# The start of a one-core encoder kernel: GpSimd's low parts of a token pair's sums wait for VectorE's scales and weight splits

## The chip, the cores and the metric

The kernel runs on one core of a Trainium2 chip. The metric is the device time of one execution in microseconds (us). TensorE is called PE here, VectorE DVE, ScalarE ACT, GpSimd POOL, SyncE SP, as in the rows of the profile.

## What is computed

A one-layer encoder over 1280 tokens (a sequence of 256 and one of 1024) of width 1024, in float32:

```python
x = x + 0.5 * swiglu(rmsnorm(x, norm_ffn1), w_ffn1_gate, w_ffn1_up, w_ffn1_down)   # d_ff 2816
x = x + hybrid_mixer(rmsnorm(x, norm_mix), ...)       # windowed attention and gated linear attention
x = x + 0.5 * swiglu(rmsnorm(x, norm_ffn2), w_ffn2_gate, w_ffn2_up, w_ffn2_down)
y = rmsnorm(x, norm_final)
```

Only the first RMSNorm and the first gate product matter for this change. `rmsnorm(x, g)` is `x * rsqrt(mean(x*x) + 1e-6) * g`.

## The kernel before

All float32 products are made of three matmuls on split operands: a high part, rounded to the type that PE multiplies, and a low part, which is the value less its high part (high by high, high by low, low by high). The gate and up products use a seven-product scheme for 2 by 2 blocks (GP1 to GP7), so PE needs not only the four blocks of the normalized tokens but also four sums of blocks, t1 to t4 (they feed GP5, GP6, GP7 and GP4).

At the beginning the 1280 tokens are ten tiles of 128, taken as five pairs (tile t and tile t+5). `PAIR_ORDER[0]` is 0, 1, 2, 3, 4. For each pair i this pipeline runs, each engine going through its own hand-written list strictly in order, with semaphores between engines:

- ACT, `norm_squares` (L1111): the sum of squares of each tile. POOL, `norm_roots` (L980, L983): two small instructions for each tile that turn it into the scale factor.
- DVE, `norm_scales` (L1580): tokens by factor by gain, one instruction of 128x1024 for each tile. PE, `norm_turn` (L2126): 8 transposes for each tile into PSUM.
- ACT, `norm_blocks` (L1123 to L1127): four evictions. DVE, `norm_blocks` (L1592 to L1613): seven instructions of 128x512, which are the sums t1 to t4 into `first_t` (L1601, L1606, L1608, L1613) and three low parts of blocks (L1592), all with one input in PSUM.
- ACT, `norm_sums` (L1133): the high part of each sum. POOL, `norm_t_lo` (L994): its low part, one instruction of 128x512 on two SBUF inputs for each sum, t1 to t4. They count on the semaphore `t_low`.

There is one set of t1 to t4 for all pairs. So DVE's `norm_blocks` of pair i may write sum j only when POOL has read it for pair i-1:

```python
def t_free(j):
    if i:
        dve.wait_ge(t_low[f], 4 * (i - 1) + j)
```

Between these stand the preparations of the first weight blocks, `g_prepare(0, s)` on DVE: the low part of weight block s (L1623, counted on `B["lo"]`) and, for s = 0 and s = 2, sums of weight blocks (L1636, L1638, L1642, counted on `B["summed"]`: 2 after s = 0, 3 after s = 2), all with two inputs in SBUF. DVE's list is: scales of pairs 0 and 1, blocks 0, scales 2, prepare 0, blocks 1, scales 3, prepare 1 and 2, blocks 2, scales 4, prepare 3 and 4, blocks 3, three evictions of gate products, blocks 4, and then the steady loop. ACT's list is: squares 0 and 1, then for each i blocks i, squares i+2, sums i, and after the sums its part of the same weight blocks (L1153); after the sums of pair 3 it evicts the first gate product (`first_p`, L1163). POOL's list is: roots 0, 1, 2, then for each i the low parts of pair i and the roots of pair i+3.

PE's list is: transposes of pairs 0 to 3, gate products 0, 1 and 2 over pairs 0 to 2 (columns c = 0), transposes of pair 4, the other products. Transposes of pair 3 wait for the end of DVE's blocks 2, those of pair 4 for the end of blocks 3. Product GP6 (step 1, c = 0) waits for POOL's second low part of pair 2, and GP2 (step 2) for ACT's eviction of GP1:

```python
if f == 0 and i >= 2:
    pe.wait_ge(N["lo"], 7 * max(1, i if i > 2 else 1))
```

SP loads x and the first three weight units at the very beginning; a later weight load waits until DVE has counted a weight block (L576).

Of the kernel before, what the change touches and what calls it, by code (L numbers as in the profile page):

```python
# [87 lines left out]
HT = TT // 2  # L88
# [61 lines left out]
def build(nc, x_prompt, x_sample, norm_ffn1, w_ffn1_gate, w_ffn1_up, w_ffn1_down, norm_mix, w_in, attn_sink,  # L150
# [4 lines left out]
    with ctx:  # L155
# [183 lines left out]
        def h_piece(f, j, e, pair):  # L339

            if f == 0:
                return hs[:, j, e, pair, :]
            if pair < 2:
                return hs2_first[:, 2 * j + e, pair, :]
            return hs2_last[:, pair - 2, :] if j + e == 0 else hq[:, 3 * (2 * j + e - 1) + pair - 2, :]
# [76 lines left out]
        def named(prefix, names):  # L422
            return {k: sem(f"{prefix}_{k}") for k in names.split()}
# [7 lines left out]
        B = named("block", "summed hi lo")  # L431
# [530 lines left out]
        def _(pool):  # L962
# [13 lines left out]
            def root(n, t, at=None):  # L976
                N = NORMS[n]
                at = t if at is None else at
                pool.wait_ge(N["sum"], at + 1)
                nc.gpsimd.tensor_scalar(ssq[:, n, t:t + 1], ssq[:, n, t:t + 1], EPS, 1.0, ALU.add, ALU.mult  # L980
                                        ).then_inc(N["root"], 1)
                pool.wait_ge(N["root"], 2 * at + 1)
                nc.gpsimd.tensor_tensor(rstd[:, n, t:t + 1], ssq[:, n, t:t + 1], expo[:, 0:1], ALU.pow  # L983
                                        ).then_inc(N["root"], 1)

            def norm_roots(f, i):
                for e in range(2):
                    root(2 * f, N_TILES[f][2 * i + e], 2 * i + e)

            def norm_t_lo(f, i):  # L990
                pair = PAIR_ORDER[f][i]
                for j, b in enumerate((GP5, GP6, GP7, GP4)):
                    pool.wait_ge(NFF[f]["hi"], 8 * i + 4 + j + 1)
                    nc.gpsimd.tensor_tensor(h_piece(f, b, 1, pair), SUMS[f][j + 1][:, :], h_piece(f, b, 0, pair).bitcast(F32),  # L994
                                            ALU.subtract).then_inc(t_low[f], 1)

            for i in range(3):
                norm_roots(0, i)
            for i in range(HT):
                norm_t_lo(0, i)  # L1000
                if i + 3 < HT:
                    norm_roots(0, i + 3)

            def g_gate(f, s, c):
                q, j = divmod(s, NP)
# [56 lines left out]
            for i in range(HT):  # L1062
                norm_roots(1, i)
                if i:
                    norm_t_lo(1, i - 1)
            norm_t_lo(1, HT - 1)
            for s, c in GORDER:
                g_gate(1, s, c)
# [1523 lines left out]
```

## Time and profile before

| what | us |
|---|---|
| median of 3 runs | 2313.0 (2310.67 to 2313.32) |
| the profiled execution | 2310.25 |
| its span | 2308.3 |
| TensorE clock granted, mean | 0.987 of full |

The span begins with the first instruction; what is around it is 1.95 us. The stretch that the change touches is the first 65 us of the span. The profile's timeline gives for each instruction, or run of like instructions, the start, the time and in brackets how long the engine sat idle before it and for whom. The windows view gives busy time of each engine within a stretch and the granted PE clock (1.00 is 2.4 GHz, 0.50 is 1.2 GHz).

### The profile page before, as it was taken

How to read it: one execution, taken by the hardware profiler on the slowest of the kernel's cores; microseconds unless marked ns; L12 is line 12 of the kernel's file. 1: busy time of each engine (PE TensorE's matmuls, PEld its weight loads, DVE VectorE, ACT ScalarE, POOL GpSimd, SP SyncE). 2: the span in 40 equal slices, each digit the busy share in tenths (PEclk: the TensorE clock that was granted, in tenths of full speed). 3: DMA queues.
4: the chain of work that ended last, by engine and by line, in shares of the span. 5: the costliest groups of instructions: out<-in, count | busy, mean ns of one | idle time of the engine just before them, and what ended most of it. 6: DMA issues, size and time to landing. Idle time of an engine off the chain costs nothing. (4 is left out here: it accounts for less than half of the span.)

```text
span 2308.3 us, 35188 instructions
## 1 busy us (share of the span) xinstructions
PE 2225.7 (96%) x13488; PEld 2004.7 (87%) x13488; DVE 1422.6 (62%) x2373; ACT 812.0 (35%) x1566; POOL 313.7 (14%) x296
## 2 busy tenths in 40 slices
PE   4999999999999999999999989899999999999998
PEld 3999999999888887776778767799999999988887
DVE  7655565565575776665655774765555555557576
ACT  6323222222333446544442211532322222233343
POOL 5100011000100002100011222521111111110000
PEclk7999999999999999999999999999999999999999
DMA  3222322322785655523335863122232232277554
GB/s 129 79 93 77 95 90 88 108 81 77 272 267 166 201 159 149 177 63 99 97 105 154 252 200 100 73 80 92 77 95 89 89 108 82 78 275 264 166 191 167
DMA packets 247141, 306.10 MB, mean 133 GB/s; under 512 B 24128, under 2 KB 159808, under 8 KB 246976
## 3 DMA queue, kind: packets, MB, share of 16 engines
q1 hardware_dynamic: 236608, 282.88, 38.7%
q10 hardware_dynamic: 10368, 20.98, 2.4%
q8 instruction: 109, 1.79, 0.3%
q14 instruction: 56, 0.46, 0.1%
HBM read 209.43 MB, written 91.10 MB: 130 GB/s over the span
## 5 line engine op out<-in xcount | busy, mean ns | idle before, releaser
L2162 PE MATMUL ps<-hs,w_hi 128*128 128x384 f32 (+1 forms) x1232 | 380.6, 309 | 3.6 <-DVE first_u L1671 2.1
L2163 PE MATMUL ps<-hs,w_hi 128*128 128x384 f32 (+1 forms) x1232 | 380.1, 309 | 0.0
L2164 PE MATMUL ps<-hs,w_lo 128*128 128x384 f32 (+1 forms) x992 | 306.1, 309 | 0.0
L2172 PE MATMUL ps<-w_hi,dh 128*128 128x512 f32 x770 | 300.7, 390 | 2.0 <-DVE w_lo L1725 0.8
L2174 PE MATMUL ps<-w_hi,dh 128*128 128x512 f32 x770 | 299.7, 389 | 0.0
L1623 DVE TENSOR_TENSOR w_lo<-w_raw,w_hi 128x512 fp32r<-128x512 f32 x178 | 133.3, 749 | 179.1 <-ACT w_hi L1153 176.7
L2173 PE MATMUL ps<-w_lo,dh 128*128 128x512 f32 x610 | 237.3, 389 | 0.0
L2162 PEld LDWEIGHTS ps<-hs,w_hi 128*128 128x128 f32 x1232 | 233.1, 189 | 4.5 <-issue 4.5
L1153 ACT CAST w_hi<-w_raw 128x512 fp32r<-128x512 f32 x220 | 135.7, 617 | 283.7 <-PE ps L2164 280.9
L2163 PEld LDWEIGHTS ps<-hs,w_hi 128*128 128x128 f32 x1232 | 233.1, 189 | 0.0
L1722 DVE TENSOR_TENSOR dh<-dr,dh 128x640 fp32r<-128x640 f32 x154 | 126.8, 824 | 167.5 <-ACT dh L1184 167.4
L1184 ACT CAST dh<-dr 128x640 fp32r<-128x640 f32 x154 | 112.0, 727 | 281.3 <-PE ps L2174 259.9
L2163 PE MATMUL ps<-hq,w_hi 128*128 128x384 f32 x616 | 206.2, 335 | 0.0
L2164 PEld LDWEIGHTS ps<-hs,w_lo 128*128 128x128 f32 x992 | 187.6, 189 | 0.0
L2162 PE MATMUL ps<-hq,w_hi 128*128 128x384 f32 x528 | 177.1, 335 | 0.8 <-DVE second_u L1671 0.8
L2162 PE MATMUL ps<-hs_first,w_hi 128*128 128x256 f32 x616 | 174.0, 282 | 3.8 <-DVE hq_f L1566 2.8
L2163 PE MATMUL ps<-hs_first,w_hi 128*128 128x256 f32 x616 | 174.2, 283 | 0.0
L2172 PEld LDWEIGHTS ps<-w_hi,dh 128*128 128x128 f32 x770 | 144.5, 188 | 33.4 <-DVE dh L1722 1.6
L2174 PEld LDWEIGHTS ps<-w_hi,dh 128*128 128x128 f32 x770 | 144.5, 188 | 30.1
L2093 PE MATMUL ps<-h_hi,w_hi 128*128 128x512 f32 (+1 forms) x432 | 161.7, 374 | 4.7 <-ACT q_rot L1266 2.5
L2095 PE MATMUL ps<-h_hi,w_lo 128*128 128x512 f32 (+1 forms) x432 | 154.2, 357 | 0.0
L2094 PE MATMUL ps<-h_lo,w_hi 128*128 128x512 f32 (+1 forms) x432 | 154.2, 357 | 0.0
(259 smaller groups left out, 4621.1 us busy)
## 6 DMA issues: line engine op xcount, KB each, us to landing
dr<-hid_mid SPq DMA_DIRECT2D x154, 320.0 KB, 3.3
w_raw<-in_w_ffn_down SPq DMA_DIRECT2D x176, 256.0 KB, 3.5
hid_mid<-st SPq DMA_DIRECT2D x88, 320.0 KB, 2.2
w_raw<-in_w_ffn_gate SPq DMA_DIRECT2D x44, 512.0 KB, 5.2
w_raw<-in_w_ffn_up SPq DMA_DIRECT2D x44, 512.0 KB, 5.1
hid_mid<-sg SPq DMA_DIRECT2D x66, 320.0 KB, 2.2
hq<-o_mid SPq DMA_DIRECT2D x60, 128.0 KB, 3.3
w_raw<-in_w_in SPq DMA_DIRECT2D x14, 512.0 KB, 4.9
```

Source lines behind the costliest of these rows:

```text
L1153: nc.scalar.copy(g_block(s)[0], src).then_inc(B["hi"], 1)
L1623: v.tensor_tensor(lo, src, hi.bitcast(F32), ALU.subtract).then_inc(B["lo"], 1)
L1722: v.tensor_tensor(a_lo, DR[f][n % D_HID][:, :], a_hi.bitcast(F32), ALU.subtract).then_inc(W["a_lo"], 1)
L2093: mm(out, hi, rhs_hi, start=first, stop=False)
L2094: mm(out, hi, rhs_lo, start=False, stop=False)
L2095: return mm(out, lo, rhs_hi, start=False, stop=last)
L2162: mm(out, hi[:, k, :], b_hi, start=k == 0 and j in (GP1, GP6, GP5), stop=False, skip_group_check=True)
L2163: mm(out, hi[:, k, :], b_lo, start=False, stop=False, skip_group_check=True)
L2164: last = mm(out, lo[:, k, :], b_hi, start=False, stop=k == 3, skip_group_check=True)
L2172: mm(out, hi, w_h, start=first and p in D_FRESH, stop=False, skip_group_check=True)
L2173: mm(out, hi, w_l, start=False, stop=False, skip_group_check=True)
L2174: return mm(out, lo, w_h, start=False, stop=last, skip_group_check=True)
```

## The change

Two things, both in POOL's list, both for the first norm only. For pairs 0, 1 and 2 `norm_t_lo` now first waits until DVE has prepared weight block 0, 2 or 4 (with its sums), that is, until just before DVE's blocks 1, 2 and 3. And the roots run one pair further ahead: roots 0 to 3 stand before the low parts of pair 0, and roots i+4 follow the low parts of pair i. No instruction is added or removed, and no other engine's list changes.

```diff
             def norm_t_lo(f, i):
                 pair = PAIR_ORDER[f][i]
+                if f == 0 and i < 3:
+                    pool.wait_ge(B["lo"], (1, 3, 5)[i])
+                    pool.wait_ge(B["summed"], (2, 3, 3)[i])
                 for j, b in enumerate((GP5, GP6, GP7, GP4)):
                     pool.wait_ge(NFF[f]["hi"], 8 * i + 4 + j + 1)
                     nc.gpsimd.tensor_tensor(h_piece(f, b, 1, pair), SUMS[f][j + 1][:, :], h_piece(f, b, 0, pair).bitcast(F32),
                                             ALU.subtract).then_inc(t_low[f], 1)
 
-            for i in range(3):
+            for i in range(4):
                 norm_roots(0, i)
             for i in range(HT):
                 norm_t_lo(0, i)
-                if i + 3 < HT:
-                    norm_roots(0, i + 3)
+                if i + 4 < HT:
+                    norm_roots(0, i + 4)
```

## Rows read from the trace of the kernel before

**Rows 1.** The page, part 1: busy time, share of the span, instructions

```profile
PE 2225.7 (96%) x13488; PEld 2004.7 (87%) x13488; DVE 1422.6 (62%) x2373; ACT 812.0 (35%) x1566; POOL 313.7 (14%) x296
```

**Rows 2.** Windows: stretch, its length, busy time by engine, PEclk, DMA share, GB/s

```profile
core 0: us, PE busy (x) PEld busy (x) DVE busy (x) ACT busy (x) POOL busy (x), PEclk, DMA share, GB/s
46.40:48.48 2.08, 2.08 (x9) 2.08 (x8) 2.08 (x4) 1.65 (x4) 0.00 (x0) 0.50 0.02 4
48.48:51.80 3.32, 3.32 (x19) 3.00 (x18) 3.32 (x6) 1.84 (x3) 2.08 (x2) 1.00 0.00 0
57.00:64.00 7.00, 7.00 (x51) 7.00 (x48) 5.30 (x9) 4.80 (x10) 4.47 (x4) 1.00 0.00 0
```

**Rows 3.** Waits of PE in 0 to 75 us: total, times, longest

```profile
PE ps L2126 <- DVE hs L1592: 16.4, 1, 16.4
PE ps L2162 <- ACT first_p L1163: 1.5, 2, 1.4
```

**Rows 4.** Timeline of DVE, 0 to 75 us: start, time, line, idle before

```profile
14.64 1.28 DVE L1580 SCALAR_TENSOR_TENSOR hs_f<-hs_f,rstd 128x1024 f32<-128x1024 f32 x1 [0.72 <-POOL rstd L983]
...
20.03 4.59 DVE L1580 SCALAR_TENSOR_TENSOR hs_f<-hs_f,rstd 128x1024 f32<-128x1024 f32 x2
24.55 1.76 DVE L1623 TENSOR_TENSOR w_lo<-w_raw,w_hi 128x512 fp32r<-128x512 f32 x1
26.23 1.75 DVE L1636 TENSOR_TENSOR w_sum<-w_raw 128x512 f32<-128x512 f32 x1
28.01 0.69 DVE L1638 TENSOR_TENSOR w_sum<-w_sum,w_raw 128x512 f32<-128x512 f32 x1
28.62 0.68 DVE L1601 TENSOR_TENSOR first_t<-first_t,ps 128x512 f32<-128x512 f32 x1
...
32.81 4.22 DVE L1580 SCALAR_TENSOR_TENSOR hs_f<-hs_f,rstd 128x1024 f32<-128x1024 f32 x2
...
42.95 4.24 DVE L1580 SCALAR_TENSOR_TENSOR hs_f<-hs_f,rstd 128x1024 f32<-128x1024 f32 x2
...
48.32 0.67 DVE L1601 TENSOR_TENSOR first_t<-first_t,ps 128x512 f32<-128x512 f32 x1
...
51.91 0.67 DVE L1592 TENSOR_TENSOR hs<-ps,hs 128x512 fp32r<-128x512 f32 x1
...
71.45 0.69 DVE L1636 TENSOR_TENSOR w_sum<-w_raw 128x512 f32<-128x512 f32 x1 [3.10 <-DMA w_raw<-in_w_ffn_up]
```

**Rows 5.** Timeline of POOL, 0 to 75 us

```profile
20.06 7.37 POOL L994 TENSOR_TENSOR hs<-first_t,hs 128x512 fp32r<-128x512 f32 x4
...
30.03 5.92 POOL L994 TENSOR_TENSOR hs<-first_t,hs 128x512 fp32r<-128x512 f32 x4
...
38.73 0.19 POOL L980 TENSOR_SCALAR ssq<-ssq 128x1 f32<-128x1 f32 x1
39.00 0.56 POOL L983 TENSOR_TENSOR rstd<-ssq,expo 128x1 f32<-128x1 f32 x1
...
49.72 5.01 POOL L994 TENSOR_TENSOR hs<-first_t,hs 128x512 fp32r<-128x512 f32 x4 [3.62 <-ACT hs L1133]
59.53 5.05 POOL L994 TENSOR_TENSOR hs<-first_t,hs 128x512 fp32r<-128x512 f32 x4 [4.79 <-ACT hs L1133]
```

**Rows 6.** Timeline of ACT, 0 to 75 us

```profile
25.81 0.19 ACT L1111 ACTIVATION_READ_ACCUMULATOR junk<-hs_f 128x1 f32 x1
...
38.03 0.19 ACT L1111 ACTIVATION_READ_ACCUMULATOR junk<-hs_f 128x1 f32 x1
...
45.99 0.59 ACT L1123 COPY first_t<-ps 128x512 f32<-128x512 f32 x1 [1.88 <-PE ps L2126]
...
52.54 0.47 ACT L1163 COPY first_p<-ps 128x384 f32<-128x384 f32 x1
```

**Rows 7.** Timeline of PE, 0 to 110 us

```profile
43.08 3.68 PE L2126 MATMUL ps<-ident,hs_f 128*128 128x128 f32 x16 [16.43 <-DVE hs L1592]
46.41 0.67 PE L2162 MATMUL ps<-hs,w_hi 128*128 128x384 f32 x1
...
53.16 0.41 PE L2162 MATMUL ps<-hs,w_hi 128*128 128x384 f32 x1 [1.36 <-ACT first_p L1163]
```

**Rows 8.** Waits of SP's queue, 0 to 110 us

```profile
SPq L576 <- DVE w_lo L1623: 66.3, 3, 47.5
```

## The prediction

> **What bounds the kernel now.** I read the page's part 1 first: PE is busy 96% of the span [rows 1], so what an edit is worth is read from PE's own idle stretches. The waits of PE over the first 75 us come next. The longest is 16.4 us, in which the transposes of pair 3 wait for the end of DVE's blocks 2, and a short one of 1.36 us follows, for ACT's `first_p` [rows 3, 7]. The timelines say what that wait is made of. DVE runs without a gap from its blocks 0 to the end of blocks 3 at 52.58 [rows 4], PE starts pair 3 at 43.08 [rows 7], just when DVE's blocks 2 are done (the scales behind them start at 42.95 [rows 4]), and PE starts GP2 at 53.16 [rows 7], when ACT's `first_p` of 52.54 is done [rows 6]. After that PE is busy all the time, 7.00 of 7.00 us from 57 to 64 [rows 2]. So up to about 53 us DVE's list is the critical path, and behind it PE is. What counts is how late PE's GP2 starts; that delay is carried to the end as it is.
>
> **What the change takes away.** Where DVE's two-input SBUF work lies beside POOL's low parts, both are slow. Two scales take 4.59, 4.22 and 4.24 us, while one beside nothing but small work takes 1.28 [rows 4]; with the usual overlap of 0.08 between neighbours, two take 1.20 + 1.28 = 2.48. The first weight split and the first weight sum take 1.76 and 1.75, where the next sum takes 0.69 [rows 4]. POOL's four low parts take 7.37 and 5.92 us there, and 5.01 where DVE does only blocks (49.72) [rows 5]. With every overlap gone DVE would save 2.11 + 2.14 (scales 2, block 0) + 1.74 + 1.76 (scales 3 and 4) = 7.75 us. Seven block instructions, with an input in PSUM, take 32.81 - 28.62 = 4.19 us [rows 4] whether POOL works or not, so POOL's new place costs them no speed.
>
> **What the change adds.** POOL's low parts of pair i now lie wholly beside DVE's blocks i+1, and these write the very sums that POOL still reads (`t_free`). Before, POOL was done or nearly so. Now DVE's t1 must wait for POOL's first, t4 for POOL's fourth. From POOL's start to the end of DVE's blocks it is then 5.01 us for the four (1.25 each), 0.04 for a semaphore, t4 0.60 and the last low part 0.68: 6.3 us, where DVE alone needs 4.19 + 0.08. And POOL can start later than DVE's list arrives, because the roots of the pair four ahead now stand in front of the low parts on POOL's queue; they need ACT's squares. What is queued behind the waiting POOL instruction is its own three further low parts and the next roots. DVE's blocks wait for the low parts and DVE's scales for the roots; ACT waits for neither, but its casts of the sums and `first_p` follow DVE's blocks.
>
> The schedule, instruction by instruction, from durations of rows 4 to 7:
>
> *Round 1.* Scales 2 start at 20.03 as now and end at 22.51; block 0 with its two sums takes to 24.43 (now 28.70). ACT is not touched so far, so its last square of pair 3 comes at 25.81 + 0.19 = 26.00 [rows 6]. POOL then does a root, 0.19 + 0.56 with gaps [rows 5], to 26.90. Its four low parts run from 26.93 to 31.94. DVE's blocks 1 end at 33.26. The scales behind them start at 33.18, now 32.81: later by 0.37. All that was gained (4.25) and more is spent in waiting from 24.43 to 28.23 for the first low part and between the sums.
>
> *Round 2.* ACT's casts follow DVE's t4, so the squares of pair 4 end 0.37 later than 38.22 [rows 6], at 38.59. DVE does scales 3 in 2.48 and three weight instructions and is ready at 37.46. POOL does the roots to 39.49 and only then starts pair 1's low parts: 39.52 to 44.53. Blocks 2 end at 45.85, the next starts at 45.77, now 42.95 [rows 4]: later by 2.82.
>
> *Round 3.* No roots stand here. Scales 4 and two weight splits take 2.40 + 1.20 + 0.08 from 45.77, to 49.45; POOL's wait ends there, its low parts run from 49.50 to 54.51, and blocks 3 end at 55.83, now 52.58 [rows 4]: later by 3.25. PE's pair 3 starts at 45.90, ACT's copies of it at 48.8 (2.91 behind PE, as 45.99 is behind 43.08 [rows 6, 7]), which is before POOL's first low part at 50.76 and so decides nothing. GP1 follows PE's transposes by 3.33, at 49.23, and with GP6 it takes 5.4 us, 46.41 to 51.80 now [rows 2, 7], so to 54.6. GP6, the second half of that, needs POOL's second low part of pair 2, out at 52.0: in time. ACT's last cast and then `first_p` move with DVE's t4, to an end of 56.25, and GP2 starts at 56.40 in place of 53.16: **3.24 us later**.
>
> *Behind it.* Pair 3's low parts on POOL go from 54.5 to 59.6, before pair 4's, which were at 59.53 with 4.79 of idle time in front [rows 5] and move to 62.8; nothing is added. Nothing absorbs the 3.24 either: the next weight loads are issued when DVE has counted a block (SP waited 66.3 us in all at L576 for DVE [rows 8]), and so DVE's wait of 3.10 us for such a load at 71.45 [rows 4] moves along with everything else. I take 3.2 us as the whole effect.
>
> Bounds: if POOL's four take 5.92 [rows 5] as with one neighbour slow, each of three rounds is 0.9 longer, and 3.2 becomes 5.9. On the other side, what I take for semaphore gaps and the order of the small roots could be 0.3 less a round, which gives 2.3. I take the fast figure since 49.72 has DVE in exactly the work that will stand beside it.
>
> **Rivals.** *The overlap alone counts (faster).* If POOL's start didn't hold DVE, the list would be shorter by up to 7.75 us: 2313.0 - 7.75 = 2305.3. For it speaks that DVE is without a gap now; against it stands that the waits are in DVE's code and that ACT's squares come at 26.00 and 38.22 whatever DVE does. It decides at POOL's first low part: it would have to start by about 23.3, and a root before it needs a square of 26.00. The Trainium skill, page "SBUF — State Buffer", section "SBUF: two separate sides", calls the pair of ports that DVE and POOL share an exclusive lock, held for the whole instruction. By that rule each of DVE's eight two-input instructions would be held once for a whole low part of 1.25 us, which makes the gain 10.0 and this rival 2303.0; the rows lie below that, with 7.75.
>
> *PE's clock stays low (slower).* PE runs at 0.50 (1.2 GHz) up to 48.48 and at 1.00 (2.4 GHz) behind it, 5.4 us after the transposes of pair 3 began [rows 2, 7]. PE stands idle for 2.8 us longer now, and between GP6 and GP2 for 1.8 in place of 1.36. If the rise comes only after GP2 has begun, a matmul costs twice the 0.175 us (19 in 3.32 [rows 2]) that it takes at the full clock. The 24 matmuls of GP1 and GP6 then take 8.4 us from 49.2 and end at 57.6, 1.2 after GP2 would start, and GP2 with its 12 costs 2.1 more: 3.2 + 1.2 + 2.1 = 6.5 us, 2319.5. It decides at 56.4. Against it: a rise 5.4 us after 45.9 is at 51.3, and the gap of 1.36 us in the trace did not bring the clock down.
>
> *The change does nothing.* If the counts that POOL now waits for were always there, 2313.0 would stay. They aren't: POOL starts at 20.06, the count comes at 24.43.
>
> **How the numbers follow.** The profiled execution took 2310.25 us, span 2308.3 and 1.95 around it; with the change it would take 2313.5. The median of the runs is 2.75 above it, and the difference goes on top of the median: 2313.0 + 3.2 = 2316.2. Chances: this forecast 0.80 (with its bounds 2.3 to 5.9), clock rival 0.07, overlap rival 0.04, nothing 0.04, the rest for something unseen. 0.2% is 4.6 us, about what a measurement can tell from no change. The forecast lies within it, with a spread of runs of 2.65 us; a quarter of its weight falls over the line. So: faster 0.05, same 0.70, slower 0.25. The range takes the bounds 2.3 and 5.9 and some 1.3 of spread on each side: 2314.0 to 2320.2; I widen the lower end to 2312.8, for the runs' own median may come out lower.
>
> **What would show it.** DVE's scales and first weight split without the slow rows (1.28 and 0.69), DVE idle in front of L1601 for POOL's L994 in blocks 1 (near 3.8 us), 2 (near 3.4) and 3 (near 1.3), and idle between the sums; POOL's L994 at 26.9, 39.5 and 49.5 with 5.0 us for four; PE's L2126 of pair 3 at 45.9 and GP2 at 56.4. Wrong it would be if POOL's low parts take other than 1.25 beside blocks, if DVE's blocks 2 end before 43, or if PE's idle time behind 57 us shrinks by what came in front.

## The result and the profile after

| | before | after |
|---|---|---|
| median of 20 runs | 2312.2 us (2309.94 to 2319.32) | 2315.55 us (2313.52 to 2320.66) |
| profiled execution, span | 2310.25, 2308.3 | 2314.80, 2312.8 |

The ratio of after to before is 1.0015, with a 95% interval of 1.0009 to 1.0021: some 3.4 us slower (2.1 to 4.9), less than the 0.2% line but clear of zero. 2316.2 had been forecast.

In the changed kernel all lines behind the change stand three lower (L1580 is L1583, L1601 is L1604, L994 is L997, L2126 is L2129, L2162 is L2165). The timeline of DVE answers to rows 4:

```profile
20.08 2.47 DVE L1583 SCALAR_TENSOR_TENSOR hs_f<-hs_f,rstd 128x1024 f32<-128x1024 f32 x2
22.47 0.68 DVE L1626 TENSOR_TENSOR w_lo<-w_raw,w_hi 128x512 fp32r<-128x512 f32 x1
...
27.93 0.69 DVE L1604 TENSOR_TENSOR first_t<-first_t,ps 128x512 f32<-128x512 f32 x1 [3.45 <-POOL hs L997]
...
32.81 2.47 DVE L1583 SCALAR_TENSOR_TENSOR hs_f<-hs_f,rstd 128x1024 f32<-128x1024 f32 x2
...
40.39 0.69 DVE L1604 TENSOR_TENSOR first_t<-first_t,ps 128x512 f32<-128x512 f32 x1 [3.31 <-POOL hs L997]
...
45.27 2.47 DVE L1583 SCALAR_TENSOR_TENSOR hs_f<-hs_f,rstd 128x1024 f32<-128x1024 f32 x2
...
50.35 0.69 DVE L1604 TENSOR_TENSOR first_t<-first_t,ps 128x512 f32<-128x512 f32 x1 [1.40 <-POOL hs L997]
...
54.69 0.68 DVE L1595 TENSOR_TENSOR hs<-ps,hs 128x512 fp32r<-128x512 f32 x1
```

All three pairs of scales take 2.47 now, in place of 4.59, 4.22 and 4.24 [rows 4], and the first split 0.68 in place of 1.76. In front of each of the three blocks DVE now sits idle for POOL: 3.45, 3.31 and 1.40 us. Compare where the scales start. Scales 3 start at 32.81, to the hundredth where they started before; scales 4 at 45.27 in place of 42.95; blocks 3 end at 55.37 in place of 52.58. The timeline of POOL says why, and answers to rows 5:

```profile
26.12 0.55 POOL L983 TENSOR_TENSOR rstd<-ssq,expo 128x1 f32<-128x1 f32 x1
26.64 4.93 POOL L997 TENSOR_TENSOR hs<-first_t,hs 128x512 fp32r<-128x512 f32 x4
...
38.58 0.56 POOL L983 TENSOR_TENSOR rstd<-ssq,expo 128x1 f32<-128x1 f32 x1
39.10 4.93 POOL L997 TENSOR_TENSOR hs<-first_t,hs 128x512 fp32r<-128x512 f32 x4
49.03 9.95 POOL L997 TENSOR_TENSOR hs<-first_t,hs 128x512 fp32r<-128x512 f32 x8 [4.99 <-DVE w_hi L1626]
```

The low parts of pairs 0 and 1 start right behind the last root of the pair ahead (26.12, 38.58), not when DVE has its weight block ready (24.48 and 37.09). Only in round 3, at 49.03, is it the new wait that releases them. PE, and PE's clock in the stretches around GP2 (columns: stretch, its length, PE busy, PEclk, DMA share, GB/s):

```profile
45.41 3.67 PE L2129 MATMUL ps<-ident,hs_f 128*128 128x128 f32 x16 [20.26 <-DVE hs L1595]
...
55.95 0.41 PE L2165 MATMUL ps<-hs,w_hi 128*128 128x384 f32 x1 [1.92 <-ACT first_p L1166]
...
59.67 1.91 PE L2129 MATMUL ps<-ident,hs_f 128*128 128x128 f32 x16
```

```profile
54.00:56.00 2.00, 0.08 (x2) 1.00 0.00 0
56.00:58.00 2.00, 2.00 (x7) 0.56 0.03 8
58.00:60.00 2.00, 2.00 (x10) 0.59 0.00 0
60.00:62.00 2.00, 2.00 (x19) 1.00 0.00 0
```

GP2 starts at 55.95, 2.79 later than before [rows 7]. But then, in this execution, PE's clock is at 1.2 GHz for most of 56 to 60, after an idle time of 1.92 us; GP2 takes 3.72 us until pair 4's transposes begin at 59.67. In the trace of before these began at 55.32, 2.16 behind GP2. So this one pair of profiles shows 2.79 of DVE's list and 1.56 of clock, 4.35 us, at pair 4. First and last start of a down product on PE, in before and then in after:

```profile
L2172 PE MATMUL ps<-w_hi,dh x770: 387/389/500, 594.9 to 2300.3; 128*128 128x512 f32 x193
```

```profile
L2175 PE MATMUL ps<-w_hi,dh x770: 387/389/498, 599.5 to 2304.7; 128*128 128x512 f32 x193
```

4.6 at the beginning of the down products, 4.4 at their end: in this pair no later stage gives any of it back. The medians lie only 3.4 apart; a second pair of profiles, below, bears on that.

### The profile page after: what moved, and what is told of

Read it like the earlier page. It is cut to its first block and busy times, and to the rows that moved or that the text cites. A ratio compares the mean times of both kernels' runs of the same rounds, so it can differ in the third digit from the quotient of the medians.

```text
span 2312.8 us, 35191 instructions
## 1 busy us (share of the span) xinstructions
PE 2225.9 (96%) x13488; PEld 2005.1 (87%) x13488; DVE 1415.9 (61%) x2373; ACT 811.8 (35%) x1566; POOL 308.2 (13%) x296
## 5 line engine op out<-in xcount | busy, mean ns | idle before, releaser
L2165 PE MATMUL ps<-hs,w_hi 128*128 128x384 f32 (+1 forms) x1232 | 381.1, 309 | 4.6 <-DVE first_u L1674 2.2
L2165 PEld LDWEIGHTS ps<-hs,w_hi 128*128 128x128 f32 x1232 | 233.2, 189 | 5.9 <-issue 5.8
L2165 PE MATMUL ps<-hq,w_hi 128*128 128x384 f32 x528 | 177.1, 335 | 0.8 <-DVE second_u L1674 0.8
L2165 PE MATMUL ps<-hs_first,w_hi 128*128 128x256 f32 x616 | 174.1, 283 | 3.8 <-DVE hq_f L1569 2.8
```

What stands on the lines that cost most here:

```text
L2165: mm(out, hi[:, k, :], b_hi, start=k == 0 and j in (GP1, GP6, GP5), stop=False, skip_group_check=True)
```

## The experiments

The theory: the waits free DVE of the overlap, as meant, but DVE may not write the one set of sums before POOL has read it; and the roots that were put ahead of POOL's low parts hold these back by another 2 us in the first two rounds. Rivals: the waits alone are the cost; the roots cost nothing; the fall of PE's clock is the cost.

| run | GP2 on PE starts | idle before | pair 4 starts | ratio to before (95%) |
|---|---|---|---|---|
| before, two profiles | 53.16, 53.29 | 1.36, 1.48 | 55.32, 55.45 | 1 |
| after, two profiles | 55.95, 56.04 | 1.92, 1.84 | 59.67, 58.23 | 1.0015 (1.0009 to 1.0021) |
| waits only | 52.46 | 1.93 | 54.65 | 0.9994 (0.9985 to 1.0003) |
| roots only | 56.94 | 3.48 | 60.92 | 1.0020 (1.0011 to 1.0029) |
| first wait only | 53.76 | 1.78 | 55.92 | 1.0002 (0.9993 to 1.0011) |
| after, two sets | 49.3 | none | 51.42 | 0.9986 (0.9977 to 0.9995) |
| after, second set for pair 1 | 51.58 | 1.91 | 53.74 | 0.9990 (0.9981 to 0.9998) |
| after, two sets, two waits | 51.34 | 2.87 | 54.95 | 0.9993 (0.9985 to 1.0002) |
| before, two sets | 53.02 | 1.93 | 56.16 | 1.0001 (0.9992 to 1.0010) |
| after, gap filled | 56.2 | filled | 58.37 | 1.0027 (1.0018 to 1.0036) |
| after, 11 matmuls at 33 us | 56.05 | 1.93 | 59.45 | 1.0033 (1.0020 to 1.0045) |

### The waits alone

```diff
+                if f == 0 and i < 3:
+                    pool.wait_ge(B["lo"], (1, 3, 5)[i])
+                    pool.wait_ge(B["summed"], (2, 3, 3)[i])
```

> The three waits of the change, with the roots left where the kernel before has them (three pairs ahead). Theory (the cost comes from POOL's start being held by the roots of the next pair, not from the waits as such): pair 0's low parts start at 24.5 in place of 26.6, blocks 1 end near 30.8, pair 1's low parts start near 35.3, blocks 2 end near 41.6, blocks 3 near 52.0, GP2 starts near 52.5: 0.65 us earlier than before (53.16), time between 2311 and 2312, ratio to before 0.9997. Rival (the waits alone cost, because DVE's blocks are held by POOL's low parts): blocks 3 end 2.8 us later than before, GP2 near 56, ratio 1.0012 or more.

Its DVE, and PE's GP2:

```profile
26.28 0.69 DVE L1604 TENSOR_TENSOR first_t<-first_t,ps 128x512 f32<-128x512 f32 x1 [1.43 <-POOL hs L997]
...
31.16 2.48 DVE L1583 SCALAR_TENSOR_TENSOR hs_f<-hs_f,rstd 128x1024 f32<-128x1024 f32 x2
...
41.75 2.48 DVE L1583 SCALAR_TENSOR_TENSOR hs_f<-hs_f,rstd 128x1024 f32<-128x1024 f32 x2
...
52.46 0.42 PE L2165 MATMUL ps<-hs,w_hi 128*128 128x384 f32 x1 [1.93 <-ACT first_p L1166]
```

DVE waits 1.43, 1.43 and 1.41 us in front of the three rounds' blocks, the time of POOL's first low part (some 1.2) and the semaphores, and another 0.5 between the sums. Scales 3 start 1.65 us before those of after, scales 4 3.5 before. GP2 comes at 52.46 where 52.5 was expected, 0.7 before the kernel before. The ratio, 0.9994, is not clear of 1; it is clear of the rival's 1.0012. The waits as such don't cost: in each round they give about as much as they take.

### The roots alone

Against the kernel before:

```diff
-            for i in range(3):
+            for i in range(4):
                 norm_roots(0, i)
...
-                if i + 3 < HT:
-                    norm_roots(0, i + 3)
+                if i + 4 < HT:
+                    norm_roots(0, i + 4)
```

> The roots one pair further ahead, without the waits. Theory: the roots of pair 3 hold POOL's low parts of pair 0 until 26.6, those of pair 4 hold pair 1's until 39.1, so rounds 1 and 2 are as in the changed kernel (scales 4 at 45.3) and only round 3 has the old overlap back; blocks 3 end near 54.9, GP2 starts near 55.4, 2.3 us later than before, and more where PE's clock falls in the gap; ratio 1.0010 to 1.0017. Rival (the waits cost, the order of the roots nothing): GP2 at 53.2, ratio 1.0000.

The same two engines:

```profile
28.02 0.69 DVE L1601 TENSOR_TENSOR first_t<-first_t,ps 128x512 f32<-128x512 f32 x1 [3.44 <-POOL hs L994]
...
45.36 4.52 DVE L1580 SCALAR_TENSOR_TENSOR hs_f<-hs_f,rstd 128x1024 f32<-128x1024 f32 x2
49.81 1.77 DVE L1623 TENSOR_TENSOR w_lo<-w_raw,w_hi 128x512 fp32r<-128x512 f32 x1
...
56.94 0.66 PE L2162 MATMUL ps<-hs,w_hi 128*128 128x384 f32 x1 [3.48 <-ACT first_p L1163]
```

Up to scales 4 (45.36 against 45.27) this is the changed kernel: the roots hold POOL there whether it waits for DVE or not (its low parts start at 26.73 and 39.19, in the changed kernel at 26.64 and 39.10). Round 3 cost more than I expected, for POOL's low parts of pair 2 now lay beside the scales and also beside a weight split (1.77), so GP2 came at 56.94 and not at 55.4; the gap in front of it grew to 3.48 us, the clock fell and pair 4 came at 60.92. The ratio of 1.0020 is above the 1.0010 to 1.0017 expected, and the rival's 1.0000 is out. Together with the run before this one: the loss of the change is that of its roots.

### A second set of sums

POOL's hold on DVE is taken away by writing t1 to t4 of pairs 1 and 3 elsewhere, into the places of tokens that are already scaled (for pair 3 DVE first waits until all of them are).

```diff
+        SET_B = (1, 3)
...
+        def sums(f, i):
+            return [SUMS[0][0]] + set_b[i] if f == 0 and i in SET_B else SUMS[f]
...
+                if f == 0 and i in (3, 4) and i - (2, 1)[i - 3] in SET_B:
+                    act.wait_ge(t_low[0], 4 * (i - (2, 1)[i - 3]) + 4)
...
-                    if i:
-                        dve.wait_ge(t_low[f], 4 * (i - 1) + j)
+                    if i and (f or i not in SET_B):
+                        last = i - 2 if f == 0 and i - 1 in SET_B else i - 1
+                        dve.wait_ge(t_low[f], 4 * last + j)
+                    elif i == 3:
+                        dve.wait_ge(N["scaled"], 2 * HT)
```

> The changed kernel with a second set of t1 to t4 for pairs 1 and 3 (in the places of tokens already scaled), so that DVE's blocks 1, 2 and 3 need not wait for POOL's low parts of the pair before. Theory (what the change gives in speed of the scales and splits is spent in waiting for the one set of sums): blocks 1 start at 24.4, blocks 2 end near 39, blocks 3 near 47.4, GP2 starts at 48 to 49, that is 4 to 5 us before the kernel before; ratio 0.9980 to 0.9984. Rival (DVE's list is held by the roots or by ACT, not by the sums): GP2 no earlier than 53, ratio 0.9997 or more.

Its DVE, then what now waits for POOL on ACT and on PE:

```profile
24.28 0.68 DVE L1615 TENSOR_TENSOR first_s<-first_t,ps 128x512 f32<-128x512 f32 x1
...
28.46 4.17 DVE L1591 SCALAR_TENSOR_TENSOR hs_f<-hs_f,rstd 128x1024 f32<-128x1024 f32 x2
...
39.61 3.60 DVE L1591 SCALAR_TENSOR_TENSOR hs_f<-hs_f,rstd 128x1024 f32<-128x1024 f32 x2
```

```profile
54.54 0.59 ACT L1134 COPY first_t<-ps 128x512 f32<-128x512 f32 x1 [2.42 <-POOL hs L1003]
```

```profile
47.14 0.41 PE L2176 MATMUL ps<-hs,w_hi 128*128 128x384 f32 x1 [2.01 <-POOL hs L1003]
```

DVE goes on at 24.28 without a wait, scales 4 start 5.7 us before those of after, and pair 4 on PE at 51.42, 3.9 before the kernel before. The overlap is back in part (4.17, 3.60), as POOL's late start now meets the next scales. POOL is the next bound: PE waits 2.01 for it, and ACT 2.42 at the wait that the second set needs; by the product that starts at 73.35 in before and at 71.19 here, 2.2 of the 3.9 are left. The ratio, 0.9986, is just short of the 0.9980 to 0.9984 expected: the mechanism is confirmed, its size was a little too high, since I had left POOL out as the next bound. This is the fastest kernel of the study, 3.3 us under before. It keeps the new order of the roots, and POOL starts pair 0 at 26.85 in it; two sets with the roots where they were was not run.

With the second set for pair 1 alone (`SET_B = (1,)`), one hold is left, that on blocks 3:

> The changed kernel with a second set of t1 to t4 for pair 1 alone, so that DVE's blocks 1 and 2 are free of POOL, and blocks 3 wait for it as in the changed kernel. Theory (the wait for the sums is the price, round by round): scales 4 start near 39.6 as with two sets for both pairs, POOL's low parts of pair 2 start at 44.5, blocks 3 end near 50.8, GP2 near 51.3; ratio 0.9990 to 0.9994. Rival (the gain of the run with two sets came from pair 3): ratio 1.0 or more.

Scales 4 and the start of blocks 3 on its DVE:

```profile
39.79 3.59 DVE L1591 SCALAR_TENSOR_TENSOR hs_f<-hs_f,rstd 128x1024 f32<-128x1024 f32 x2
...
45.98 0.69 DVE L1615 TENSOR_TENSOR first_t<-first_t,ps 128x512 f32<-128x512 f32 x1 [1.39 <-POOL hs L1003]
```

Blocks 3 wait 1.39, as in after, GP2 comes at 51.58 and the ratio is 0.9990: both as forecast.

Without the new waits and roots, the second sets should be worth nothing, because DVE never waited for POOL in the kernel before:

> The kernel before (no new waits, roots three pairs ahead) with the second set of t1 to t4 for pairs 1 and 3. Theory: DVE had no idle time for POOL before, so the second set gives nothing: scales 2, 3 and 4 stay at 4.2 to 4.6 us, blocks 3 end near 52.6, GP2 starts near 53.2, ratio between 0.9995 and 1.0005. Rival (the second set alone brings what the two sets brought with the change, 0.9986): ratio 0.9988 or less, GP2 before 51.

The scales 3 and 4 on its DVE:

```profile
32.63 4.24 DVE L1588 SCALAR_TENSOR_TENSOR hs_f<-hs_f,rstd 128x1024 f32<-128x1024 f32 x2
42.79 4.24 DVE L1588 SCALAR_TENSOR_TENSOR hs_f<-hs_f,rstd 128x1024 f32<-128x1024 f32 x2
```

They are: 1.0001, with GP2 at 53.02. So neither half brings the 0.9986 by itself: the second sets alone give nothing, the waits alone 0.7 us at GP2, and with the new roots they lose.

### Where the overlap goes when one wait is made

Against the kernel before, the waits of the change for pair 0 only, the roots as they were:

```diff
+                if f == 0 and i < 1:
+                    pool.wait_ge(B["lo"], (1, 3, 5)[i])
+                    pool.wait_ge(B["summed"], (2, 3, 3)[i])
```

> The kernel before with the first of the three new waits alone (pair 0's low parts wait for weight block 0 and its sums), roots as before, one set of sums. Theory: the first round gains the most (scales 2 and two weight instructions, 4.2 us) and pays the least (POOL can start at 24.5 to 25.0, right when DVE is ready), so scales 3 start near 31.2 in place of 32.8, and rounds 2 and 3 run as before, 1.6 us earlier; GP2 near 51.5, ratio 0.9991 to 0.9995. Rival (each round pays what it gains): GP2 near 53, ratio 0.9998 or more.

Its DVE from scales 3 to scales 4, blocks 2 left out:

```profile
30.70 3.49 DVE L1583 SCALAR_TENSOR_TENSOR hs_f<-hs_f,rstd 128x1024 f32<-128x1024 f32 x2
34.12 1.75 DVE L1626 TENSOR_TENSOR w_lo<-w_sum,w_hi 128x512 fp32r<-128x512 f32 x1
35.79 1.75 DVE L1626 TENSOR_TENSOR w_lo<-w_raw,w_hi 128x512 fp32r<-128x512 f32 x1
37.47 1.74 DVE L1645 TENSOR_TENSOR w_raw<-w_raw 128x512 f32<-128x512 f32 x1
...
43.32 4.47 DVE L1583 SCALAR_TENSOR_TENSOR hs_f<-hs_f,rstd 128x1024 f32<-128x1024 f32 x2
```

I was wrong on this one. Scales 3 do start early (30.70, 2.1 before the kernel before), but POOL's low parts of pair 1, which had lain half beside DVE's blocks 1 (they started at 30.03, the blocks ended at 32.89), start at 31.25, behind those blocks' end, and now lie beside three weight instructions, each 1.1 us slower. Scales 4 start at 43.32, later than before, and the ratio is 1.0002. The gain of a round can be taken back by the next one: moving DVE's list against POOL's moves the overlap, it doesn't take it away.

The same shows when the third wait is left out of the kernel with two sets (`i < 2` in place of `i < 3`):

> The run with two sets of sums without the third of the new waits. There PE waited 2.0 us at GP6 for POOL's low parts of pair 2, and ACT 2.4 us for those of pair 3. Theory: POOL starts pair 2 at 42.1 in place of 44.5; scales 4 and the splits get slower by about 1.5 us, first_p ends near 50, GP2 starts near 50, and pair 4's blocks are not held, so the time is the same as with the third wait or a little less: ratio 0.9983 to 0.9988. Rival (the old overlap costs more than it gives): 0.9992 or more.

POOL's low parts of pair 2, and GP2 on PE:

```profile
42.04 6.91 POOL L1003 TENSOR_TENSOR hs<-first_t,hs 128x512 fp32r<-128x512 f32 x4
...
51.34 0.41 PE L2176 MATMUL ps<-hs,w_hi 128*128 128x384 f32 x1 [2.87 <-ACT first_p L1174]
```

POOL starts pair 2 at 42.04 in place of 44.49, but takes 6.91 for it, and slows DVE's two weight splits to 1.77 each (0.68 with the third wait): GP2 comes at 51.34 and not at 50, 2.0 later than with the third wait. The ratio, 0.9993, is the rival's; but its interval overlaps that of the run with three waits (0.9986), so that the third wait is worth having here rests on the two profiles alone.

### The clock in the gap

> The kernel before, profiled a second time. Theory: its gap of 1.36 us between GP6 and GP2 leaves PE's clock at 1.0, so GP2 at 53.2, transposes of pair 4 at 55.3, first down matmul near 595 as in the first profile. Rival (the clock falls in that gap or not by chance, and the first profile of before was a lucky one): pair 4 at 56.5 or later with PE at 0.5 from 53 on.

> The changed kernel, profiled a second time. Theory: the gap of 1.9 us lets PE's clock fall again, GP2 takes 3.7 us, pair 4 at 59.7. Rival (chance): clock at 1.0, GP2 takes 2.2 us, pair 4 at 58.1.

The second profile of before, then that of after, timeline of PE and PE's window around GP2:

```profile
53.29 0.41 PE L2162 MATMUL ps<-hs,w_hi 128*128 128x384 f32 x1 [1.48 <-ACT first_p L1163]
```

```profile
56.04 0.41 PE L2165 MATMUL ps<-hs,w_hi 128*128 128x384 f32 x1 [1.84 <-ACT first_p L1166]
58.23 1.91 PE L2129 MATMUL ps<-ident,hs_f 128*128 128x128 f32 x16
```

```profile
56.00:58.00 2.00, 1.96 (x11) 1.00 0.03 8
```

GP2 stands at the same place again (55.95 and 56.04; 53.16 and 53.29), so 2.8 us is a firm part of the difference. The clock is not: after a gap of 1.84 us it stays at 1.00 this time, and GP2 takes 2.19. Over all the runs without extra matmuls, it fell behind two of the six gaps of 1.78 to 1.93 us ahead of a GP2, behind both longer ones (2.87 and 3.48), and behind neither of 1.36 and 1.48. Two traces of before are too few to say that it never falls there. Nor is the gap set by the change alone: the run with the second sets alone has DVE's list of before and a gap of 1.93, because PE's clock rose 4.3 us after the start of pair 3's transposes (5.4 in before) and GP1 with GP6 took 4.85 us in place of 5.39; and behind that gap the clock fell too. So how much of the median's 3.4 us is clock is not shown; the 2.8 of the list alone lies within 2.1 to 4.9.

The down products in this second pair, before and then after:

```profile
L2172 PE MATMUL ps<-w_hi,dh x770: 387/389/500, 595.9 to 2304.3; 128*128 128x512 f32 x193
```

```profile
L2175 PE MATMUL ps<-w_hi,dh x770: 387/389/499, 598.1 to 2305.9; 128*128 128x512 f32 x193
```

The 2.8 of pair 4 are 2.2 at their beginning and 1.6 at their end. But the two profiles of before, 0.1 apart at pair 4, are 1.0 and 4.0 apart there. Single profiles show that the delay reaches the later stages, not that the last microsecond of it does.

To fill the gap, PE gets matmuls whose product nobody reads:

```diff
-            for j in range(3):
+            for j in range(2):
                 g_step(0, j, 0)
+            for _ in range(11):
+                mm(ps[:, 3, 0:3 * P], g_block(0)[0][:, 0, :], h_cols(0, GP1, 0, 0, 0), start=True, stop=True, ...)
+            g_step(0, 2, 0)
```

> The changed kernel with 11 more matmuls of 128x384 on PE between GP6 and GP2 of the first pairs, into a free bank, whose product nobody reads. They fill the 1.9 us in which PE waits for first_p. Theory (in that idle time PE's clock falls to 0.5, which makes GP2 take 3.7 us in place of 2.2): with the gap filled the clock stays at 1.0, transposes of pair 4 start near 58.1 in place of 59.67, time 1.5 us under the changed kernel, ratio to before 1.0008. Rival (the fall of the clock has another cause than the gap, or costs nothing at the end): ratio as the changed kernel's, 1.0015, pair 4 at 59.7.

Its timeline of PE, and PE's windows around GP2:

```profile
58.37 1.91 PE L2129 MATMUL ps<-ident,hs_f 128*128 128x128 f32 x16
...
77.37 0.55 PE L2165 MATMUL ps<-hs,w_hi 128*128 128x256 f32 x1 [2.52 <-DVE first_u L1674]
```

```profile
54.00:56.00 2.00, 2.00 (x13) 1.00 0.00 0
56.00:58.00 2.00, 1.98 (x12) 1.00 0.03 8
```

In its own place the filler did as forecast: the clock stayed at 1.00 and pair 4 came at 58.37. But the second profile of after kept its clock without a filler (58.23), so this trace alone doesn't show that the filler did it. The whole did not do as forecast: 1.0027. At 77.37 PE waits 2.52 us, 0.8 more than in after, behind a weight load that took 4.8 us to land (4.0 in after), and there the clock does fall. So I moved the same 11 matmuls to where PE has nothing to do, against the changed kernel:

```diff
-            for i in range(4):
+            for i in range(3):
                 norm_turn(0, i)
+            pe.wait_ge(N1["lo"], 14)
+            pe.wait_ge(B["lo"], 1)
+            for _ in range(11):
+                mm(ps[:, 3, 0:3 * P], g_block(0)[0][:, 0, :], hs[:, GP1, 0, 0, 0:3 * P], start=True, stop=True, ...)
+            norm_turn(0, 3)
```

> The changed kernel with the same 11 extra matmuls as in the run that filled the gap, but at about 33 us, in PE's long idle time ahead of the transposes of pair 3, where they hold nothing. The filled gap kept the clock up and had pair 4 start 1.3 us earlier, yet the whole took 3 us more. Theory 1 (the loss of that run comes from what PE and the weight load met there, a load that landed 0.8 us later and the clock falling in that wait, not from the extra instructions): here the time is the changed kernel's, ratio to before 1.0015. Theory 2 (extra instructions on PE's list cost by themselves): ratio 1.0025 or more.

The extra matmuls on PE, and PE's wait behind the weight load:

```profile
33.02 3.63 PE L2225 MATMUL ps<-hs,w_hi 128*128 128x384 f32 x11 [7.96 <-DVE hs L1595]
...
79.14 0.36 PE L2165 MATMUL ps<-hs,w_hi 128*128 128x256 f32 x1 [2.86 <-DVE first_u L1674]
```

Pair 3 still starts at 45.49 and GP2 at 56.05, yet the ratio is 1.0033 (five runs), some 4 us over the changed kernel's, and the same load takes 5.2 us. Eleven matmuls that hold nothing in their own place make later work slower. The ratio is the one of theory 2, and theory 1 is out as I meant it: the slow load came again, wherever the matmuls stood.

The traces show what the two runs with extra matmuls share. In each of the 13 traces one fetch of instructions (a packet of 0.02 MB on DMA queue q8) falls between 70 and 85 us. In the eleven without extra matmuls it comes after the load has landed (78.5 and 77.5 in the two of after), and the load takes 3.8 to 4.2 us. In the two with them it comes in the same half microsecond as the load's first packets (71.5 and 73.0), and the load takes 4.8 and 5.2. PE's wait behind the load grows to 2.52 and 2.86, and the clock falls behind it: 0.68 from 75 to 80 us in the one, 0.66 from 80 to 85 in the other, where both profiles of after have 1.00. Against the second profile of after the two runs are 0.8 and 2.6 us late at the product behind the load (in the one at 33 us the clock had also fallen at GP2, 1.2) and 2.1 and 4.5 late at the first down product. So the likely reason is that more instructions move a fetch into the load. It fits all 13 traces, but no run moved the fetch by itself: it is argued, not shown.

It also means that the run with the filled gap can't say in the total what the fall of the clock costs. The two profiles of after can, up to the down products: 1.44 at pair 4 (59.67 and 58.23) and 1.4 at the first down product (599.5 and 598.1).

## Why the prediction was right

- *What bounds.* DVE's list up to 53 us and PE behind it: right. That GP2's delay is carried to the end as it is holds for the first pair of profiles; in the second 1.6 of 2.8 are left at the last down product, with as much scatter between two profiles of one kernel.
- *The gain from ended overlap.* Two scales 2.48, measured 2.47; the first split 0.69, measured 0.68.
- *The price of the wait.* 5.01 for POOL's four beside blocks, measured 4.93 (26.64, 39.10). From POOL's start to the next scales 6.25 was taken; it is 6.17. DVE idle in front of the three blocks was forecast near 3.8, 3.4 and 1.3; it was 3.45, 3.31 and 1.40.
- *The roots.* POOL's start at 26.93, 39.52 and 49.50 was forecast; it was 26.64, 39.10 and 49.03. In this execution ACT had ended its squares 0.24 earlier, at 25.76 in place of 26.00, and with 0.05 less at the root and 0.08 less in each of rounds 1 and 2 this makes GP2 2.79 later and not 3.24. The experiments confirm the step itself: without the new order of the roots the loss is gone (0.9994), with it alone it is all there (1.0020).
- *GP6.* "In time" was a little off: PE waits 0.32 for POOL (51.70). It lies within the gap before GP2 and costs nothing.
- *The clock rival.* It had 0.07, 3.3 us on top of the list and the wrong form, a late rise behind pair 3. What happens is a fall behind the gap that I had counted (1.8 us, in place of 1.36) and dismissed because 1.36 had done no harm. It cost 1.56 us in one of the two profiles of after and nothing in the other. The rise, which I put 5.4 us behind the start of pair 3 from the one trace, came 4.0 and 5.4 behind it in the two of after.
- *The size.* 3.2 was forecast and 3.4 measured, with an interval of 2.1 to 4.9; that they lie so close is in part luck, for the list is 0.45 less than forecast and a clock that falls in some executions may make up for it.
- *The overlap rival.* 7.75 us of overlap is what DVE would save, and the forecast was right that the list can't have it: even with two sets of sums the kernel gains 3.3.
- *The lock.* The Trainium skill, page "SBUF — State Buffer", section "SBUF: two separate sides", gives an exclusive lock for a whole instruction. A two-input DVE instruction beside POOL is about 1.1 us longer here, somewhat under POOL's 1.25 (1.75 for 0.68, by the three rows at 34 to 39 us of the run with the first wait only). The trace agrees with the rule in kind; the size is best taken from rows.

## What to carry to other kernels

Before an engine is held back to keep it out of another's way, look for the buffer that ties them: if the held engine frees what the other will write next, the wait comes back on the other side. Here a second buffer took the changed kernel from 1.0015 to 0.9986, and the old order of the roots took it to 0.9994; the two together were not run. When a small step is put ahead of a long one on an in-order engine, look at what the small one itself waits for: two roots of 0.8 us held four low parts by 2 us, twice. And a list shifted against another takes its overlap along, so count the next rounds too.

## What the runs showed of the hardware

PE's clock fell from 2.4 to 1.2 GHz behind an idle time of 1.9 us in one execution and not in another of the same kernel (1.92 and 1.84 us, pair 4 at 59.67 and 58.23); behind 2.87 and 3.48 it fell both times. Its rise varies too: 4.0 and 5.4 us behind the start of the same transposes in these two executions. Beside a POOL instruction with two SBUF inputs a 128x512 DVE instruction with two SBUF inputs took 1.75 us in place of 0.68, and one with an input in PSUM 0.68 as always. And 11 matmuls in idle time on PE made the kernel 4 us slower than without them, with a weight load landing in 5.2 us in place of 4.0; in both runs with such matmuls an instruction fetch falls together with the start of that load, and in none of the others. That the fetch is the cause is not shown.
